# Two attentions in a fused two-layer kernel: both heads of a pair in one step, unsplit scores on half the rows each

## The chip, the cores and the metric

One core of a Trainium2 chip runs one program. The metric is the device time of one execution in microseconds (us), here the median of three runs. The engines are named as in the profile: PE is TensorE's matmul side, PEld its weight loads, DVE is VectorE, ACT is ScalarE, POOL is GpSimd, SP is the engine whose queue issues most of the DMAs.

## The reference, cut to what matters

Two layers follow each other on a sequence of 1024 tokens of width 1024, all in fp32. Each layer projects the tokens, runs several mixers, merges them and ends in an MLP. Each layer has one attention among its mixers:

```python
# layer 1, "fox": 8 heads of 64
for blk in range(L // Q_BLOCK):                       # 8 blocks of 128 queries
    q0 = blk * Q_BLOCK; kend = q0 + Q_BLOCK
    s = jnp.einsum('bqhd,bkhd->bhqk', q[:, q0:kend], k[:, :kend]) * scale
    s = s + cum[:, :, q0:kend, None] - cum[:, :, None, :kend]
    s = jnp.where(k_pos[None, :] <= q_pos[:, None], s, NEG_INF)
    outs.append(jnp.einsum('bhqk,bkhd->bqhd', jax.nn.softmax(s, axis=-1), v[:, :kend]))
# layer 2, "band": 4 heads of 64, chunks of 64 queries, each with the chunk itself and 8 chunks to its left
s = einsum(q, k of the band) * scale + rel_bias[dist];  o = softmax(s) @ v of the band
```

## The kernel before

Almost all of the arithmetic is large products: a weight tile of 128x128 against the activations, 128x1024. Weights and activations are split into a high part in fp32r and a remainder (`w_hi`, `w_lo`, `act_hi`, `act_lo`), and a tile takes six matmuls of 128x512 in fp32r (L322): three products of parts for two halves. Eight tiles are a unit. At the start of a unit ACT casts the next unit's weights (L278), POOL forms the remainder (L282), and when a row of eight tiles is done, DVE evicts it (L609) and SP stores it to DRAM (L611).

The mixers run inside these products. Class `Woven` holds a generator of tiles; `point(n)` in the mixer's code lets it emit as many tiles as the mixer's progress is worth, so that PE's queue holds product tiles between the mixer's own matmuls. `w.again(points, kept)` says over how many points the tiles that are left (but `kept`) are to be spread. For fox these are 384 - 137 = 247 tiles over 8*28+11 = 235 points, for band 143 tiles over 4*28+12 = 124 points. Every engine works through its queue in the order in which the code emits it.

`attention` is used by both. It goes head by head, and in each head over eight query blocks n; a step is one query block of one head. For fox the keys of block n are the first 128(n+1); for band they are 128(n+1) up to n=3 and 640 from n=4. A step does this:

- Scores (L818): q has been cast to fp32r (`qh`, L735) with a remainder `ql` (L736). k lies twice in `ks`: its high part on partitions 0 to 63, its remainder on 64 to 127 (L741, L742), since both halves of `raw_qk` hold the head. Two fp32r matmuls with all 128 rows, `qh` and `ql` against `ks`, so give the score of a head for up to 512 keys. They write `wide`, two PSUM banks.
- DVE adds the bias while it reads `wide` (`add_bias`: L884 and L886 in fox, L920 in band), takes the row maximum (L832) and negates it (L833). ACT takes the exponential with the row sum (L836).
- One step later DVE inverts the sum (L767) and ACT scales the row (L768).
- Two steps later PE transposes the probabilities in groups of up to four blocks into `bank[0]` (L638), and ACT copies each group out (L642). The even head's go to `pe`, which holds a whole head; the odd head's go to `pt`, and right behind them the product with the values follows for both heads (L786), fp32 with 64 columns of the array for each head. So there are 32 groups of L786 in fox and 16 in band. Three buffers of scores `s[:, t % 3]` hold the steps under way.
- `values` transposes v once for each pair (L751), `gather` copies four blocks of output (L794).

`fetch(h + 1)` is issued when head h begins. In fox the bias row of a head is a row of `fox_cum` broadcast over all partitions (`fx_cb`, 512 KB in SBUF, double-buffered, L859), and POOL makes the masked diagonal blocks `fx_own` out of it (L873). A short convolution (`short_conv`) takes up DVE with one instruction each step.

Other mixers of the kernel use fp32 matmuls, unsplit. Three of them matter here. L373 (`row_sums`) multiplies 128 rows and 128 columns by 512: four matmuls in the code. L1244 and L1289 have 64 rows each, two of them on partitions 0 to 63 and then two on 64 to 127, and the two halves write different PSUM banks:

```python
for g in range(2):
    rows_g = slice(S5_P * g, S5_P * (g + 1))
    for c in (RE, IM):
        nc.tensor.matmul(ps[g][:, o:o + CH], cl[rows_g, pr, c, 1:, :]..., state[rows_g, c, pr, :], ...)
```

L1289 loads 128 columns of weights, L1244 16. Both stream 128 columns.

Of the kernel before, what the change touches and what calls it, by code (L numbers as in the profile page):

```python
# [9 lines left out]
P = 128  # L10
# [117 lines left out]
def _build(nc, ctx, t, out):  # L128
# [38 lines left out]
    qk_in = Count(sem("qk_in"))  # L167
# [523 lines left out]
    def attention(heads, tiles, src, rows, stored, mixed, row0, head_bias, add_bias, name, beside, first_queue=nc.sync):  # L691
# [8 lines left out]
        halves = src.rearrange("b (h p) n -> (b h) p n", h=2)  # L700
        with ExitStack() as at:
            raw_qk, raw_v = sb(at, name + "x", [P, 2, L]), sb(at, name + "v", [P, L])
            qh, ql, ks = (sb(at, name + n, [P, 2, L], F32R) for n in ("qh", "ql", "ks"))
            vt = sb(at, name + "vt", [P, NT, P])
            bias, bias_in, bias_fixed = head_bias(at)
            keys = [(k1 - k0) // P for q0, k0, k1 in tiles]
            s, pe = sb(at, name + "s", [P, 3, L]), sb(at, name + "pe", [P, sum(keys), P])
            pt, o, st = sb(at, name + "pt", [P, NT, P]), sb(at, name + "o", [P, L]), sb(at, name + "st", [P, 3, 2])

            arrived, bias_ready, split, scores, biased, values_in, weighed = {}, {}, {}, {}, {}, {}, {}  # L710
            v_read = {}

            def fetch(h):

                queue = SP if h else first_queue
                if h:
                    SP.wait_ge(*split[h - 1])
                for n in range(3):
                    queue.wait_ge(*stored[rows[n] + h // 2])
                for n in range(2):  # L720
                    for half in range(2):
                        arrived[h] = qk_in.mark(queue.dma_start(raw_qk[half * HD:(half + 1) * HD, n, :],
                                                             halves[h + 2 * rows[n]]))
                if h % 2 == 0:
                    if h:
                        SP.wait_ge(*v_read[h - 2])
                    v_in.mark(queue.dma_start(raw_v[:], src[h // 2 + rows[2]]))
                if h > 1:
                    SP.wait_ge(*biased[h - 2])
                bias_in(h)  # L730

            def prepare_q(h):

                sl = h % 2
                a_q = A.mark(A.after(arrived[h], scores.get(h - 2)).copy(qh[:, sl, :], raw_qk[:, 0, :]))  # L735
                V.mark(V.after(a_q).tensor_tensor(ql[:, sl, :], raw_qk[:, 0, :], qh[:, sl, :].bitcast(F32), ALU.subtract))  # L736

            def prepare_k(h):

                sl = h % 2  # L740
                a_k = A.mark(A.after(arrived[h], scores.get(h - 2)).copy(ks[:, sl, :], raw_qk[:, 1, :]))  # L741
                split[h] = V.mark(V.after(a_k).tensor_tensor(ks[HD:P, sl, :], raw_qk[HD:P, 1, :],  # L742
                                                             ks[HD:P, sl, :].bitcast(F32), ALU.subtract))
                bias_ready[h] = bias_fixed(h)

            def values(h, copied):

                for j0 in (0, 4):
                    PE.after(v_in.last(), copied, *(() if h else entered))
                    for j in range(4):  # L750
                        last = nc.tensor.transpose(bank[0][:, j * P:(j + 1) * P], raw_v[:, (j0 + j) * P:(j0 + j + 1) * P],  # L751
                                                   ident[:])
                    ready = PE.mark(last)
                    v_read[h] = ready
                    copied = A.mark(A.after(ready, weighed.get(h - 1)).copy(
                        vt[:, j0:j0 + 4, :], bank[0][:].rearrange("p (j n) -> p j n", j=4)))
                    if j0 == 0:
                        point()
                values_in[h + 1] = copied
                return copied  # L760

            pv_done, turned, state = {}, [], {"copied": None, "o_read": None, "scores_read": None}

            def scaled(t, h, n, k0, nk, e):

                sum_, w = st[:, t % 3, 1:2], nk * P
                v = V.mark(V.after(e).reciprocal(sum_, sum_))  # L767
                return A.mark(A.after(v).activation(s[:, t % 3, 0:w], s[:, t % 3, 0:w], ACT.Copy, scale=sum_))  # L768

            def turn(t, h, n, k0, nk, e):  # L770

                few, even = nk <= 4, pe[:, sum(keys[:n]):sum(keys[:n + 1]), :]
                point((1.5 if few else 1) + (2 if n == 0 else 0))
                if t == 0:
                    PE.after(*settled)
                state["copied"] = transposes(pt[:, 0:nk, :] if h % 2 else even, lambda j: s[:, t % 3, j * P:(j + 1) * P], nk, P,
                                             e, free=state["copied"], after=lambda: point(1.5 if few else 1))
                turned.append(state["copied"])
                if h % 2 == 0:
                    point(0.5)  # L780
                    return
                PE.after(state["copied"], values_in[h], state["o_read"])
                for j in range(nk):
                    for x, p in enumerate((even, pt)):
                        mine = slice(x * HD, (x + 1) * HD)
                        last = nc.tensor.matmul(bank[1][mine, n % 4 * P:(n % 4 + 1) * P], vt[:, k0 // P + j, mine],  # L786
                                                p[:, j, :], start=j == 0, stop=j == nk - 1)
                pv_done[t] = weighed[h] = PE.mark(last)

            def gather(t, h, n):  # L790

                if h % 2 == 0 or n % 4 != 3:
                    return
                state["o_read"] = V.mark(V.after(pv_done[t], out_in.get(h // 2 - 1)).tensor_copy(  # L794
                    o[:, n // 4 * HALF:(n // 4 + 1) * HALF], bank[1][:]))
                if n == NT - 1:
                    SP.wait_ge(*V.last())
                    out_in[h // 2] = stores[0].mark(SP.dma_start(mixed[h // 2 + row0], o[:]))

            out_in = {}  # L800
            fetch(0)
            point(5)
            prepare_q(0)
            prepare_k(0)
            point(3)
            exped, ready_p = None, None
            for t, (h, n) in enumerate((h, n) for h in range(heads) for n in range(NT)):
                q0, k0, k1 = tiles[n]
                w, sl = k1 - k0, t % 3
                if n == 0:  # L810
                    if h + 1 < heads:
                        fetch(h + 1)
                    aside = beside(h)
                PE.after(split[h], state["scores_read"])
                for c in range(0, w, HALF):
                    e = min(w, c + HALF)
                    for q in (qh, ql):
                        last = nc.tensor.matmul(wide[:, c:e], q[:, h % 2, q0:q0 + P], ks[:, h % 2, k0 + c:k0 + e],  # L818
                                                start=q is qh, stop=q is ql)
                scores[h] = ready = PE.mark(last)  # L820
                if t == 0:
                    point(3)
                if ready_p:
                    turn(*ready_p)
                drained = ready_p
                if exped:
                    ready_p = (*exped[:-1], scaled(*exped))
                sc = s[:, sl, 0:w]
                V.after(ready, bias_ready[h], turned[t - 3] if t > 2 else None, *(settled if t == 2 else ()))
                state["scores_read"] = add_bias(h, n, sc, wide[:, 0:w], bias[:, h % 2, :], q0, k0, k1)  # L830
                biased[h] = V.last()
                V.mark(V.then().reduce_max(st[:, sl, 0:1], sc, AX.X))  # L832
                x = V.mark(V.then().tensor_scalar(st[:, sl, 0:1], st[:, sl, 0:1], -1.0, None, ALU.mult))  # L833
                if drained:
                    gather(*drained[0:3])
                x = A.mark(A.after(x).activation(sc, sc, ACT.Exp, bias=st[:, sl, 0:1], accum_out=st[:, sl, 1:2]))  # L836
                exped = (t, h, n, k0, w // P, x)
                if n == 3 and h % 2 == 0:
                    state["copied"] = values(h, state["copied"])
# [12 lines left out]
    def fox(stored):  # L852
# [28 lines left out]
        def add_bias(h, n, sc, psum, cb, q0, k0, k1):  # L881
# [8 lines left out]
            elif n < 2 and h:  # L890
                mask(h, n + 6)
# [1337 lines left out]
```

## Time and profile before

| | |
|---|---|
| median of 3 runs | 3460.83 us (3458.84 to 3464.54) |
| the profiled execution, device time | 3463.03 us |
| its span, first to last instruction | 3461.3 us |
| PE busy | 3366.4 us, 97% of the span |
| DVE, ACT, POOL busy | 38%, 27%, 27% |
| fox, first to last instruction of its own on PE | 313.7 to 762.6 us |
| band, the same | 1822.0 to 2065 us |

A busy share of PE counts a matmul from its start to its modelled end, and matmuls overlap, so it is high wherever matmuls follow each other closely. What a piece of work costs PE is read from the starts: how much later the products behind it begin than they would without it.

### The profile page before, as it was taken

Reading aid. Unit: us, or ns where it says so; the run is one execution under the profiler, and the core shown is the slowest. Engines: PE = TensorE matmul, PEld = TensorE weight load, DVE = VectorE, ACT = ScalarE, POOL = GpSimd, SP = SyncE. Lnnn points to the kernel's source line nnn. Section 1 sums busy time; section 2 is a strip of 40 time slices with the busy share of each in tenths; the row PEclk is TensorE's granted clock in tenths of the full one; section 3 lists DMA queues with packets and bytes.
Section 4 is the critical chain, followed back from the end, with each engine's and each line's share of the span. In section 5 each row is a group of like instructions: output and inputs, shape, how many; then the busy total and the mean of one; then the engine's idle time right before and its main releaser. Section 6 shows DMA issues by size and latency. Waiting matters only on the chain. (4 is left out here: it accounts for less than half of the span.)

```text
span 3461.3 us, 40933 instructions
## 1 busy us (share of the span) xinstructions
PE 3366.4 (97%) x16184; PEld 2739.9 (79%) x16184; DVE 1311.0 (38%) x1631; ACT 944.6 (27%) x1248; POOL 940.3 (27%) x507
## 2 busy tenths in 40 slices
PE   8999999999999999999999999999999999999997
PEld 6788888777877888888867777787878688888886
DVE  6852455434244131313143427654461521121123
ACT  3213444444232111111233332313342411111112
POOL 2212222213332222222421124231254222122125
PEclk9999999999999999999999999999999999999998
DMA  3435444235411111111233222213362211111113
GB/s 129 159 94 159 129 151 149 95 115 184 146 63 65 49 49 49 48 49 47 93 125 118 96 101 101 80 68 144 136 213 97 79 48 49 48 48 49 49 52 130
DMA packets 101603, 333.43 MB, mean 96 GB/s; under 512 B 11920, under 2 KB 21520, under 8 KB 101328
## 3 DMA queue, kind: packets, MB, share of 16 engines
q1 hardware_dynamic: 100432, 327.95, 28.3%
q10 hardware_dynamic: 1040, 3.67, 0.3%
q8 instruction: 90, 1.47, 0.2%
q14 instruction: 41, 0.34, 0.0%
HBM read 249.06 MB, written 85.52 MB: 97 GB/s over the span
## 5 line engine op out<-in xcount | busy, mean ns | idle before, releaser
L282 POOL TENSOR_TENSOR w_lo<-w_raw,w_hi 128x1024 fp32r<-128x1024 f32 (+1 forms) x304 | 694.8, 2289 | 2348.8 <-ACT w_hi L278 2299.7
L322 PE MATMUL pair<-act_hi,w_hi 128*128 128x512 f32 x2976 | 942.8, 398 | 6.5 <-DVE f1v L2000 1.5
L322 PE MATMUL pair<-act_lo,w_hi 128*128 128x512 f32 x2976 | 920.9, 391 | 0.0
L322 PE MATMUL pair<-act_hi,w_lo 128*128 128x512 f32 x2976 | 919.6, 390 | 0.0
L322 PEld LDWEIGHTS pair<-act_hi,w_lo 128*128 128x128 f32 x2976 | 559.6, 188 | 119.8
L322 PEld LDWEIGHTS pair<-act_lo,w_hi 128*128 128x128 f32 x2976 | 559.6, 188 | 119.3
L322 PEld LDWEIGHTS pair<-act_hi,w_hi 128*128 128x128 f32 x2976 | 539.9, 189 | 111.9 <-issue 10.0
L278 ACT CAST w_hi<-w_raw 128x1024 fp32r<-128x1024 f32 x274 | 287.4, 1049 | 848.4 <-PE pair L322 802.2
L609 DVE TENSOR_TENSOR p<-pair,rs 128x1024 f32<-128x1024 f32 x100 | 122.2, 1222 | 406.4 <-PE pair L322 406.3
L1943 DVE TENSOR_TENSOR f2v<-pair,rs 128x1024 f32<-128x1024 f32 x42 | 51.4, 1225 | 333.1 <-PE pair L322 333.1
L322 PE MATMUL pair<-f1hl,w_hi 128*128 128x512 f32 x480 | 147.8, 389 | 0.0
L322 PE MATMUL pair<-f1hh,w_hi 128*128 128x512 f32 x480 | 147.8, 389 | 0.0
L322 PE MATMUL pair<-f1hh,w_lo 128*128 128x512 f32 x480 | 147.7, 389 | 0.0
L441 PE MATMUL pair<-act_hi,w_hi 128*128 128x512 f32 x192 | 87.1, 453 | 26.6 <-DVE act_lo L545 13.7
L1937 DVE TENSOR_TENSOR f1v<-pair,rs 128x1024 f32<-128x1024 f32 x30 | 36.7, 1224 | 186.2 <-PE pair L322 186.2
L1932 ACT CAST f1hh<-f1v 128x1024 f32 x30 | 31.5, 1050 | 276.1 <-DVE f1v L1938 276.1
L322 PEld LDWEIGHTS pair<-f1hl,w_hi 128*128 128x128 f32 x480 | 90.1, 188 | 18.7
L322 PEld LDWEIGHTS pair<-f1hh,w_hi 128*128 128x128 f32 x480 | 90.1, 188 | 18.7
L322 PEld LDWEIGHTS pair<-f1hh,w_lo 128*128 128x128 f32 x480 | 90.1, 188 | 18.7
L1969 DVE TENSOR_TENSOR f1y<-f1y,pair 128x1024 f32 x22 | 26.9, 1221 | 201.3 <-PE pair L322 201.3
L322 PE MATMUL pair<-f2hh,w_lo 128*128 128x512 f32 x328 | 101.0, 389 | 0.0
L322 PE MATMUL pair<-f2hh,w_hi 128*128 128x512 f32 x328 | 101.0, 389 | 0.0
(486 smaller groups left out, 4042.8 us busy)
## 6 DMA issues: line engine op xcount, KB each, us to landing
w_raw<-in_stream SPq DMA_DIRECT2D x275, 512.0 KB, 3.6
proj<-p SPq DMA_DIRECT2D x101, 512.0 KB, 2.6
m2g<-proj SPq DMA_DIRECT2D x32, 512.0 KB, 4.8
m1g<-proj SPq DMA_DIRECT2D x16, 512.0 KB, 3.5
x<-f1y SPq DMA_DIRECT2D x16, 512.0 KB, 2.6
act_lo<-x SPq DMA_DIRECT2D x16, 512.0 KB, 6.9
foxx<-proj SPq DMA_DIRECT2D x28, 256.0 KB, 5.7
fx_cb<-fox_cum SPq DMA_DIRECT2D x8, 512.0 KB, 7.5
```

Of the source, the lines that this page charges most:

```text
L278: nc.scalar.copy(whi[:, slot, :], raw[:, slot, :]).then_inc(s_whi, 1)
L282: last = nc.gpsimd.tensor_tensor(wlo[:, slot, at:at + n], raw[:, slot, at:at + n], whi[:, slot, at:at + n].bitcast(F32), ALU.subtract)
L322: last = nc.tensor.matmul(out_pair[:, h * HALF:(h + 1) * HALF], wt, a[:, h * HALF:(h + 1) * HALF], start=k == 0 and n_pass == 0, stop=k == ...
L441: last = nc.tensor.matmul(out, wt, a[:, half], start=k == 0 and n_pass == 0, stop=k == self.tiles - 1 and n_pass == 2)
L609: done = read(V.after(ready, stored).tensor_tensor(buf[:, slot, :], psum[:], rs[:], ALU.mult))
L1932: a = A.mark(A.after(mark).copy(hi, x[:, s, :]))
L1937: a = read(V.then(ready).tensor_tensor(x[:, s, :], psum[:], rs[:], ALU.mult))
L1943: v = read(V.then(ready).tensor_tensor(x[:, o, :], psum[:], rs[:], ALU.mult))
L1969: done = read(V.after(ready).tensor_tensor(dst, dst, psum[:], ALU.add))
```

## The change

A step is now one query block of both heads of a pair; fox has 32 steps and band 16. q and k of the pair are loaded as they lie in DRAM, one head on partitions 0 to 63 and one on 64 to 127, and go to PE as they are, in fp32, with 64 rows for each head; the casts and remainders of q and k (L735 to L742) are gone. Each head's scores of up to 512 keys go to its own half of `wide`. A query block with more than 512 keys so has two groups of scores, the second of which (`scores(i, n, HALF)`) waits until DVE has read the first. Transposes and the product with the values follow one step behind the scores instead of two, with two buffers. In fox the own (diagonal) rows and the bias rows of a pair are loaded separately, and there is one buffer for each head of a pair: those of the next pair are loaded when the last reader in this pair is through. In band the biases of all four heads are loaded at the start. The points become 4*57+13 = 241 for fox and 2*57+13 = 127 for band; the tiles are the same.

```diff
+            def fetch(i):
+                queue = SP if i else first_queue
...
+                if i > 1:
+                    SP.wait_ge(*scored[i - 2])
                 for n in range(2):
+                    arrived[i] = qk_in[i % 2].mark(queue.dma_start(qk[:, i % 2, n, :], src[i + rows[n]]))
...
-            def prepare_q(h):
-                a_q = A.mark(A.after(arrived[h], scores.get(h - 2)).copy(qh[:, sl, :], raw_qk[:, 0, :]))
-                V.mark(V.after(a_q).tensor_tensor(ql[:, sl, :], raw_qk[:, 0, :], qh[:, sl, :].bitcast(F32), ALU.subtract))
-            def prepare_k(h):
...
+            def scores(i, n, c):
+                q0, k0, k1 = tiles[n]
+                w = min(HALF, k1 - k0 - c)
+                PE.after(arrived[i], state["scores_read"])
+                for x in range(2):
+                    head = slice(x * HD, (x + 1) * HD)
+                    last = nc.tensor.matmul(wide[:, x * HALF:x * HALF + w], qk[head, i % 2, 0, q0:q0 + P],
+                                            qk[head, i % 2, 1, k0 + c:k0 + c + w], start=True, stop=True)
+                scored[i] = ready = PE.mark(last)
+                for x in range(2):
+                    state["scores_read"] = add_bias(i, n, x, c, c + w, s[:, t % 2, x, :], wide[:, x * HALF:x * HALF + w],
+                                                    V.after(ready, turned.get(t - 2), *(settled if t < 2 else ())))
+            def turn(t, x, j0, m, ready):
+                PE.after(ready[x], state["bank"], *(settled if t == 0 else ()))
+                for j in range(m):
+                    last = nc.tensor.transpose(bank[0][:, j * P:(j + 1) * P], s[:, t % 2, x, (j0 + j) * P:(j0 + j + 1) * P],
+                                               ident[:])
+                turned[t] = PE.mark(last)
+                state["bank"] = A.mark(A.after(turned[t]).copy(
+                    pt[:, x, j0:j0 + m, :], bank[0][:, 0:m * P].rearrange("p (j n) -> p j n", j=m)))
+            def groups(n):
+                return [(x, j0, min(4, nk - j0)) for x in range(2) for j0 in range(0, nk, 4)]
...
+            for t, (i, n) in enumerate((i, n) for i in range(pairs) for n in range(NT)):
                 q0, k0, k1 = tiles[n]
+                w, total = k1 - k0, 8 if k1 - k0 > HALF else 6
...
+                scores(i, n, 0)
+                parts = groups(before[1]) if before else [None, None]
+                for g, part in enumerate(parts):
+                    if part:
+                        turn(t - 1, *part, ready)
+                    if g == 1 and w > HALF:
+                        scores(i, n, HALF)
+                    if g == (2 if len(parts) == 4 else int(w > HALF)):
+                        for x in range(2):
+                            V.mark(V.then().reduce_max(sm, sc, AX.X))
+                            exps[x] = V.mark(V.then().tensor_scalar(sm, sm, -1.0, None, ALU.mult))
+                        exps[0] = A.mark(A.after(exps[0]).activation(... ACT.Exp ...))
+                        next(aside, None)
+                    point(total / len(parts))
+                if before:
+                    weigh(*before)
+                if n == 0:
+                    values(i)
+                exps[1] = A.mark(A.after(exps[1]).activation(... ACT.Exp ...))
+                ready = []
+                for x in range(2):
+                    v = V.mark(V.after(exps[x]).reciprocal(sm, sm))
+                    ready.append(A.mark(A.after(v).activation(... ACT.Copy, scale=sm)))
+                if before:
+                    gather(*before)
+                next(aside, None)
+                bias_ahead(i, n)
+                if n == 2 and i + 1 < pairs:
+                    fetch(i + 1)
+                before = i, n
+            for part in groups(before[1]):
+                turn(t, *part, ready)
+                point(2)
+            weigh(*before)
+            gather(*before)
# fox
+            def rows(i):
+                for x in range(2):
+                    here[i] = bias_load[i % 2].mark(SP.dma_start(cb[:, x, :], fox_cum[2 * i + x].partition_broadcast(P)))
+            def ahead(i, n):
+                if n == 0 and i:
+                    SP.wait_ge(*read[i - 1, NT - 1, 1])
+                    own_rows(i, 1, edge)
+                    rows(i)
+                if n < NT - 1:
+                    mask(i, n + 1)
+                elif i + 1 < pairs:
+                    SP.wait_ge(*read[i, NT - 2, 1])
+                    own_rows(i + 1, 0, slice(0, (NT - 1) * P))
+                    mask(i + 1, 0)
+            def add(i, n, x, c, e, sc, psum, vector):
+                left, q0 = min(e, n * P), n * P
+                if left > c:
+                    v = V.mark(V.after(here[i]).scalar_tensor_tensor(sc[:, c:left], psum[:, 0:left - c], HD ** -0.5,
+                                                                     cb[:, x, c:left], ALU.mult, ALU.subtract))
...
-            w.again(FOX_HEADS * 28 + 11, 2 * KT)
+            w.again(FOX_HEADS // 2 * 57 + 13, 2 * KT)
-                w.again(BAND_HEADS * 28 + 12, 32 * KT)
+                w.again(BAND_HEADS // 2 * 57 + 13, 32 * KT)
```

## Rows read from the trace of the kernel before

**Rows 1.** The page, busy time of PE over the whole span.

```profile
PE 3366.4 (97%) x16184; PEld 2739.9 (79%) x16184; DVE 1311.0 (38%) x1631; ACT 944.6 (27%) x1248; POOL 940.3 (27%) x507
```

**Rows 2.** Windows: stretch, its length, busy time of each engine, clock, DMA.

```profile
313.70:762.60 448.90, 442.65 (x2519) 357.69 (x2517) 206.63 (x383) 188.93 (x341) 107.05 (x88) 1.00 0.37 121
1806.00:1822.00 16.00, 12.39 (x55) 9.94 (x53) 2.50 (x3) 4.05 (x4) 4.21 (x5) 0.96 0.64 185
1822.00:2065.00 243.00, 238.00 (x1276) 191.16 (x1276) 85.71 (x163) 87.85 (x172) 47.94 (x43) 0.99 0.30 95
```

**Rows 3.** Waits of PE in fox: us in total, times, longest.

```profile
PE wide L818 <- DVE foxs L886: 3.0, 4, 1.1
```

**Rows 4.** Timeline of PE around two score groups of fox: start, duration, work.

```profile
353.78 0.39 PE L818 MATMUL wide<-foxks,foxqh 128*128 128x512 f32 x1
...
354.68 0.62 PE L322 MATMUL pair<-act_hi,w_hi 128*128 128x512 f32 x2
...
360.37 0.63 PE L322 MATMUL pair<-act_hi,w_lo 128*128 128x512 f32 x2
360.84 0.22 PE L818 MATMUL wide<-foxks,foxqh 128*128 128x128 f32 x1
...
361.01 0.68 PE L322 MATMUL pair<-act_hi,w_hi 128*128 128x512 f32 x2
361.52 0.62 PE L322 MATMUL pair<-act_lo,w_hi 128*128 128x512 f32 x2
```

**Rows 5.** Timeline of PE at fp32 matmuls with 128 rows (L373).

```profile
2355.86 3.59 PE L373 MATMUL wide<-gm_vt,ones 128*128 128x512 f32 x8
2358.89 1.03 PE L322 MATMUL pair<-act_hi,w_hi 128*128 128x512 f32 x2
2359.76 0.62 PE L322 MATMUL pair<-act_lo,w_hi 128*128 128x512 f32 x2
```

**Rows 6.** Timeline of PE at fp32 matmuls with 64 rows, 128 columns (L1289).

```profile
221.41 0.62 PE L322 MATMUL pair<-act_lo,w_hi 128*128 128x512 f32 x2
221.86 0.61 PE L322 MATMUL pair<-act_hi,w_lo 128*128 128x512 f32 x2
222.41 2.16 PE L1289 MATMUL bank<-s_state,s_first 64*128 64x128 f32 x32
224.50 0.72 PE L322 MATMUL pair<-act_hi,w_hi 128*128 128x512 f32 x2
225.06 0.63 PE L322 MATMUL pair<-act_lo,w_hi 128*128 128x512 f32 x2
```

**Rows 7.** Timeline of PE at fp32 matmuls with 64 rows, 16 columns (L1244).

```profile
207.41 0.63 PE L322 MATMUL pair<-act_hi,w_lo 128*128 128x512 f32 x2
207.97 1.93 PE L1244 MATMUL wide<-s_first,s_b 64*16 64x128 f32 x32
209.84 0.73 PE L322 MATMUL pair<-act_hi,w_hi 128*128 128x512 f32 x2
210.40 0.62 PE L322 MATMUL pair<-act_lo,w_hi 128*128 128x512 f32 x2
```

**Rows 8.** DMA issues in fox: count, size, median us from issue to landing.

```profile
fx_cb<-fox_cum SPq DMA_DIRECT2D x8, 512.0 KB, 7.5
```

**Rows 9.** Timeline of PE at the start of band.

```profile
1822.04 0.47 PE L818 MATMUL wide<-bandks,bandqh 128*128 128x128 f32 x1 [3.65 <-DVE bandks L742]
...
1823.48 1.05 PE L322 MATMUL pair<-act_lo,w_hi 128*128 128x512 f32 x2
1824.34 1.05 PE L322 MATMUL pair<-act_hi,w_lo 128*128 128x512 f32 x2
```

**Rows 10.** Lines by form in fox, ACT and DVE: count, busy us, mean ns.

```profile
L836 ACT ACTIVATE foxs<-foxs,foxst 128x256 f32<-128x256 f32 x8 | 4.0, 503 | 2.3 <-DVE foxst L833 2.1
L836 ACT ACTIVATE foxs<-foxs,foxst 128x1024 f32<-128x1024 f32 x8 | 9.1, 1144 | 4.1 <-DVE foxst L833 4.1
L886 DVE SCALAR_TENSOR_TENSOR foxs<-wide,fx_own 128x128 f32<-128x128 f32 x64 | 17.9, 280 | 1.7 <-POOL fx_own L864 1.6
L832 DVE TENSOR_REDUCE foxst<-foxs 128x1 f32<-128x256 f32 x8 | 3.4, 420 | 0.3
```

More of the change, by code:

```diff
@@ L1 @@
+import itertools
 import math
@@ L699, in attention @@
         NT = L // P
-        halves = src.rearrange("b (h p) n -> (b h) p n", h=2)
         with ExitStack() as at:
-            raw_qk, raw_v = sb(at, name + "x", [P, 2, L]), sb(at, name + "v", [P, L])
-            qh, ql, ks = (sb(at, name + n, [P, 2, L], F32R) for n in ("qh", "ql", "ks"))
+            qk, raw_v = sb(at, name + "x", [P, 2, 2, L]), sb(at, name + "v", [P, L])
             vt = sb(at, name + "vt", [P, NT, P])
[L705 to L717, printed above, removed]
+            bias_first, bias_ahead, add_bias = head_bias(at)
@@ L720, in fetch @@
                 for n in range(2):
[L721 to L729, printed above, removed]
@@ L746, in values @@
-            def values(h, copied):
+                    arrived[i] = qk_in[i % 2].mark(queue.dma_start(qk[:, i % 2, n, :], src[i + rows[n]]))
+                if i:
+                    SP.wait_ge(*v_read[i - 1])
+                v_in.mark(queue.dma_start(raw_v[:], src[i + rows[2]]))
+            def values(i):
                 for j0 in (0, 4):
-                    PE.after(v_in.last(), copied, *(() if h else entered))
-                    for j in range(4):
-                        last = nc.tensor.transpose(bank[0][:, j * P:(j + 1) * P], raw_v[:, (j0 + j) * P:(j0 + j + 1) * P],
+                    PE.after(v_in.last(), state["bank"], *(() if i else entered))
+                    for j in range(j0, j0 + 4):
+                        last = nc.tensor.transpose(bank[0][:, (j - j0) * P:(j - j0 + 1) * P], raw_v[:, j * P:(j + 1) * P],
@@ new lines, in weigh @@
+            def weigh(i, n):
+                q0, k0, k1 = tiles[n]
+                nk = (k1 - k0) // P
+                PE.after(state["bank"], copied[i], state["o_read"])
+                for j in range(nk):
+                    for x in range(2):
+                        head = slice(x * HD, (x + 1) * HD)
+                        last = nc.tensor.matmul(bank[1][head, n % 4 * P:(n % 4 + 1) * P], vt[:, k0 // P + j, head],
+                                                pt[:, x, j, :], start=j == 0, stop=j == nk - 1)
+                weighed[i] = PE.mark(last)
@@ L801, in attention @@
+            def groups(n):
+                q0, k0, k1 = tiles[n]
+                nk = (k1 - k0) // P
+                return [(x, j0, min(4, nk - j0)) for x in range(2) for j0 in range(0, nk, 4)]
             fetch(0)
+            bias_first()
             point(5)
[L803 to L807, printed above, removed]
+            before, ready = None, None
@@ L820, in attention @@
[L820 to L839, printed above, removed]
@@ L840, in attention @@
-                if n == 4 and h + 1 < heads:
-                    prepare_q(h + 1)
-                if n == 5 and h + 1 < heads:
-                    prepare_k(h + 1)
-                next(aside, None)
-            turn(*ready_p)
-            gather(*ready_p[0:3])
-            ready_p = (*exped[:-1], scaled(*exped))
-            point(1)
-            turn(*ready_p)
-            gather(*ready_p[0:3])
+                    aside = itertools.chain(beside(2 * i), beside(2 * i + 1))
+                scores(i, n, 0)
@@ L894, in fox @@
+            return first, ahead, add
         with ExitStack() as at:
-            attention(FOX_HEADS, [(n * P, 0, (n + 1) * P) for n in range(8)], proj1, (Q_, K_, V_), stored, mixed1, 8,
-                      head_bias, add_bias, "fox", short_conv(at, stored), nc.scalar)
+            attention(pairs, [(n * P, 0, (n + 1) * P) for n in range(8)], proj1, (Q_, K_, V_), stored, mixed1, 8,
+                      head_bias, "fox", short_conv(at, stored), nc.scalar)
     def band(beside, stored):
+        pairs = BAND_HEADS // 2
```

161 lines of the change are left out of this document (66 added, 95 removed).

## The prediction

> **What bounds the kernel now.** I read the page first. PE is busy 97% of the span and no other engine more than 38% (PEld, the weight loads, runs beside PE) [rows 1], so the question for every edit is what it does to PE. Then I read the windows over the two attentions. In fox PE stands idle for 448.90 - 442.65 = 6.25 us, in band for 243.00 - 238.00 = 5.0 us, and just before band's first score for 16.00 - 12.39 = 3.6 us [rows 2]. Everything else, 11.3 us apart, is PE working through its queue: the product tiles that are woven in cover the softmax chain. The largest group of waits on PE in fox is only 3.0 us, four waits for DVE to empty `wide` [rows 3]. So ACT and DVE work that the change removes (the casts and remainders of q and k, four instructions a head) is hidden work. It can give back no more than a part of those 11.3 us. What counts is what the new matmuls cost PE, read from starts in the timeline.
>
> **Pitch of a pass.** A product pass of 512 columns starts 0.228 us after the one before: two from 221.41 to 221.86 [rows 6]. That is the clock's upper level, 2.4 GHz, which the window shows as 1.00. An fp32 matmul costs more. L373 is four matmuls in the code and eight records in the trace, so one fp32 matmul is two passes. From 2355.86 to 2359.76 lie those eight and two product passes: (3.90 - 0.46) / 8 = 0.43 us for a pass of 512 columns [rows 5]. An fp32 matmul of 512 columns therefore takes 0.86 us, four times 1/2.4 GHz a column, with nothing added before or behind. In the sums below a pass is 0.43/512 = 0.00084 us a column in fp32 and half of that in fp32r.
>
> **Scores before.** Four fp32r passes of 512 columns (one head, 1024 keys) take 354.68 - 353.78 = 0.90 us [rows 4], 0.225 each, with no cost of switching. Two of 128 columns take 361.52 - 360.37 = 1.15 less four product passes, 0.91: 0.24 us, which is 0.13 more than their columns. For a pair of heads of fox that is 2 heads x 2 passes x 4608 keys (128 times 1 to 8) x 0.225/512 = 8.1 us plus four groups of 128 keys x 0.13, 8.6 us; four pairs, 34.5 us. Band has 3840 keys a head: 6.75 + 10 x 0.13 = 8.05 us a pair, 16.1 us for two. Before: 50.6 us.
>
> **Scores after, the columns.** Each head is now one fp32 matmul, two passes of 0.00084 us a column, with 64 rows. No score of the kernel before is of this form, but L1289 and L1244 are: fp32, 64 rows, alternate halves of the partitions, different banks. L1289's 32 records of 128 columns last 2.16 us in all [rows 6]; one after the other they would take 32 x 0.107 = 3.4 us. They fit 16 slots of 0.107, that is 1.7 us: the two halves run side by side. So I take both heads of a pair for the price of one: 2 passes x 4608 x 0.00084 = 7.74 us a pair, 31.0 in fox; 2 x 3840 x 0.00084 = 6.45 a pair, 12.9 in band. Together 43.9 us. This alone would be 6.7 us less than before.
>
> The Trainium skill, "TensorE: Matmul & The Clock Gate", section "The mechanism", says that matmuls start and end strictly in the order of the program, even on different row groups. The first rival takes that up from the rows.
>
> **Scores after, the switch.** A group with 64 rows costs PE more than its slots. L1289: from 221.86 to 225.06 are 3.20 us, less four product passes 2.29, less 16 slots 0.57 us too much [rows 6]. L1244 in the same way: 2.99 - 0.91 - 1.72 = 0.36 us [rows 7]. The two differ in the columns of weights they load, 128 and 16. The new scores load 128, but their passes are mostly long enough to hide the second load, which 128-column slots aren't (L1289's excess includes that). So 0.57 for the groups of 128 keys down to about 0.4 for the longer ones; I take 0.435 a group on the mean, with 0.36 and 0.57 as bounds. Below nothing is excluded: every group in this form in the trace has the excess. The groups are 12 a pair (one for each of eight blocks, a second for the four with more than 512 keys): 48 in fox, 24 in band, 72 x 0.435 = 31.3 us (25.9 to 41.0). Scores after: 43.9 + 31.3 = 75.2 us. The term is 75.2 - 50.6 = **+24.6 us** (+19.2 to +34.3).
>
> **Transposes, values, output.** The number and size of transposes (L638), of products with the values (L786), of their groups and of the switches to 64 columns for them are the same: 0 us. Tiles are the same number too, 247 and 143; spread over 241 points instead of 235 they come to 1.03 a point.
>
> **Lag of one step.** With every step the scaled probabilities must be ready when PE reaches the next step's first transpose. Take a small step: behind the last transposes stand three points, 3.1 tiles of six passes, 4.2 us; then the values of the block before and the next scores, 1.7 us or more. ACT's second exponential and both scalings stand in the queue behind the last copy, 0.5 us each at 256 keys [rows 10], so they are through inside the tiles. Only where a unit of weights begins at the very end of the tiles does the cast get in ahead of them, and that costs under 1 us. In the largest step, 1024 keys, two points (2.8 us) and then the values and the next scores stand over a copy, an exponential of 1.14 us [rows 10] and a scaling that I take as equally long, some 3.1 us. I take 2 us for all steps together (0 to 6). What is queued behind these waits on PE is the next tiles, nobody else.
>
> **What goes.** Of the 11.3 us of idle [rows 2], the waits for `wide` at 256 to 384 keys, the ones at v's transposes and the tails, where two whole steps were turned without enough tiles between, lose their cause: -9 us. The 3.6 us before band stay. There PE waited for q and k, then for their splitting [rows 9]. The splitting (about 4 us) goes, but three points of tiles (3.4 tiles, 4.7 us) that stood ahead of the first scores now stand behind them, so PE reaches them as much earlier and waits for the load itself. The half clock that followed (two product passes 0.86 us apart instead of 0.46, level 1.2 GHz [rows 9]) I take to stay too: 0 us.
>
> **What comes: bias rows at the change of pair in fox.** This edit moves a load from a head ahead to the moment of use. `rows(i)` goes out at the end of the pair's first step. SP must first pass the store of the output, which waits for `gather`, and that for the second exponential, which stands behind the copies of v. I put the issue of the second bias row at 3.3 us after PE starts the scores of step 1, my estimate from the order of the queues, with the store and three other issues ahead of it. A bias row lands 7.5 us after its issue [rows 8], so at about 11. DVE stands at the first bias add of step 1 until then. Then four adds of 0.28, a maximum of 0.42 and its negation bring the first exponential to 12.7, 13.3 when done [rows 10]. ACT has the copy of the second head's transposes behind that exponential. PE comes to the product with the values, which needs that copy, after 0.8 of scores, 0.6 of transposes and six points (8.5 us), at 9.9 us, and waits until 13.7. That is 4 us at each of three changes of pair: **+12 us** (0 if the rows leave and land 4 us earlier, 20 if the clock falls after each wait as it did before band, where the mean clock of 0.99 over 243 us [rows 2] stands for some 5 us at half clock, 2.5 us lost).
>
> **Sum.** 24.6 + 2 - 9 + 12 = +29.6 us; against the profiled execution's 3463.0 that is 3492.6. The profiled execution lies 2.2 us above the median of the runs, so by the median 3460.8 + 29.6, **3490 us**, 0.9% slower. Its own range is 3478 to 3504: the switch between its bounds or the bias waits between theirs, not both at their ends.
>
> **Rivals.**
> Passes start strictly in order. Then of first head pass 1, pass 2, second head pass 1, pass 2 only the middle two overlap: three slots instead of two, half of 43.9 more, +22 us, 3512. For it: the program order. Against: in L1289 four records of one half come ahead of four of the other, in order that would take 24 slots, 2.6 us, and they took 2.16 [rows 6]. The Trainium skill's rule above is this rival; by it the time would be 3512, and this trace speaks against it.
> No overlap at all: another 22 us, 3534. Against it is the same row, more strongly.
> One more stall: the softmax chain no longer fits into one step and PE waits in each of the 48 steps, by 0.5 us, 24 us in all: 3514. For it is the lag; against it the slack worked out above.
> No measurable change: the switch at its lower bound and no wait for the bias, 19.2 + 2 - 9 = +12, and some 5 to 9 us more won at band's start, should the load be there when PE asks for it: 3464 to 3468.
> Faster: the switch costs nothing for passes of 512 columns. Then the scores are 6.7 us cheaper, with 9 us of idle gone and 2 us new 3447 by the median, if the bias rows come in time. The point from which it decides is a switch of 0.09 us: 72 x 0.09 - 6.7 - 9 + 2 = -7. For it: an fp32 group with 128 rows costs no switch [rows 5]. Against: rows 6 and 7.
>
> **How the numbers follow.** The forecast 0.58, strict order 0.13, no overlap 0.07, a stall in each step 0.06, no change 0.08, faster 0.08. The range leaves out no overlap, faster and half of no change, 0.19: 3466 to 3520. By 0.2% (7 us, about what a measurement of this kernel tells from no change): faster 0.08, same 0.08, slower 0.84.
>
> **What the changed profile would show.** Score groups with 64*128 shapes whose two heads' records start within 0.02 us of each other, passes 0.43 us apart at 512 columns; a group of 512 keys for both heads costing 1.3 us between products where two heads cost 0.9 before. If the second head's records start a pass later, strict order holds. PE waiting at L786's successor for ACT's copy at three places some 10 us into the second step of a pair, with DVE waiting there for the bias DMA. No other waits of PE above 1 us inside the attentions. Fox's stretch longer by about 20 us and band's by about 7. The prediction is wrong if the switch behaves otherwise for long passes than for short ones, since both rows that price it have 128 columns.

## The result and the profile after

The median went from 3460.83 us to 3479.74 us (five runs, 3474.50 to 3480.45): the ratio is 1.005, 95% interval 1.0035 to 1.0064, slower by 18.9 us. The forecast was slower, 3490 us with a range of 3466 to 3520. So the direction was right, and the loss is two thirds of the 29.6 us that were forecast.

The profiled execution is the fastest of the five, 3474.50 us, 11.5 us above that of before; the other four took 3478.9 to 3480.5 us at a mean granted clock of 0.992 instead of 0.994, which is 0.002 x 3478 / 0.5 = 14 us more at the lower level, 7 us lost. Where the sums below go by the trace, they are held against what happened inside the two attentions.

The page of the changed kernel, busy time over the span (before: [rows 1]):

```profile
PE 3375.4 (97%) x16184; PEld 2717.1 (78%) x16184; DVE 1275.0 (37%) x1645; ACT 919.7 (26%) x1224; POOL 938.5 (27%) x514
```

ACT lost 25 us of work and DVE 36 us, and the time went up: as in [rows 1], PE alone decides. The windows over the attentions (stretch, length, busy time of PE, PEld, DVE, ACT, POOL, clock, DMA; before: [rows 2]):

```profile
308.12:778.71 470.59, 457.47 (x2534) 348.12 (x2534) 183.85 (x393) 176.02 (x327) 102.26 (x95) 0.99 0.33 117
1832.52:2077.90 245.38, 243.93 (x1300) 187.86 (x1300) 79.29 (x171) 82.74 (x167) 48.27 (x43) 0.99 0.24 88
```

Fox's stretch is 21.7 us longer and band's 2.4 us, but both now begin three points of tiles (3 or 4 tiles) earlier. So I number the product tiles in both traces and measure from the start of a tile to the start of a later one. From tile 128 (260.36 us before, 258.57 after) to tile 400 (762.56 and 778.91) fox takes 18.2 us more; from tile 1120 (1804.63 and 1820.96) to tile 1296 (2119.28 and 2132.66) band takes 3.0 us less. That is +15.2 us. The difference of the two executions is 11.5, so outside the attentions the changed kernel was 3.7 us shorter: the code is the same there, but some 8 us less of it ran at half clock, which is 4 us lost less.

PE around a score group that stands between tiles, 512 keys of both heads; the three transposes ahead of it have the tiling of the product tiles. (Tiling is here the rows and columns of the array that a matmul uses, which the profile writes as 128*128, 64*128 or 128*64; a switch is what a change of it costs PE.)

```profile
402.25 0.62 PE L324 MATMUL pair<-act_hi,w_lo 128*128 128x512 f32 x2
402.71 0.49 PE L755 MATMUL bank<-ident,foxs 128*128 128x128 f32 x3
403.13 1.13 PE L744 MATMUL wide<-foxx 64*128 64x512 f32 x4
404.19 0.73 PE L324 MATMUL pair<-act_hi,w_hi 128*128 128x512 f32 x2
404.76 0.62 PE L324 MATMUL pair<-act_lo,w_hi 128*128 128x512 f32 x2
```

Four records (two passes for each head) last 1.13 us. One after the other they would need 4 x 0.43 = 1.7. The price is read as in [rows 6]: from 402.25 to 404.76 are 2.51 us, less four product passes 1.60, less 0.34 for three transposes 1.26, less 2 x 0.43 a switch of **0.40 us**. It was 0.41 for 128 keys and 0.40 for 256 and 384 in the same way.

PE around a score group that stands right behind the product with the values (L769):

```profile
349.49 0.61 PE L324 MATMUL pair<-act_hi,w_lo 128*128 128x512 f32 x2
350.04 0.88 PE L769 MATMUL bank<-foxpt,foxvt 128*64 128x128 f32 x12
350.85 1.13 PE L744 MATMUL wide<-foxx 64*128 64x512 f32 x4
351.90 0.66 PE L755 MATMUL bank<-ident,foxs 128*128 128x128 f32 x4
352.32 0.70 PE L324 MATMUL pair<-act_hi,w_hi 128*128 128x512 f32 x2
352.86 0.63 PE L324 MATMUL pair<-act_lo,w_hi 128*128 128x512 f32 x2
```

The group is the same size, 512 keys of both heads. From 349.49 to 352.86 are 3.37 us, less four product passes 2.46, less 0.45 for four transposes 2.01. The product with the values costs 1.01 by itself (it stands alone in the second experiment below), so the scores cost 1.00, and less their 0.86 the switch is **0.14 us**. The prediction priced it at 0.435 everywhere.

The first change of pair in fox. The score group of the new pair's step 1, which needs the bias rows, in PE's timeline:

```profile
430.98 0.70 PE L744 MATMUL wide<-foxx 64*128 64x256 f32 x4
```

The load of this pair's bias rows (L851), issued after that, in the timeline of SP's queue:

```profile
433.09 0.93 SPq L851 DMA_DIRECT2D fx_cb<-fox_cum  x2
```

What then waited, in the timeline of all engines (in brackets the idle time ahead and what ended it):

```profile
439.84 0.29 DVE L890 SCALAR_TENSOR_TENSOR foxs<-wide,fx_cb 128x128 f32<-128x128 f32 x1 [7.59 <-DMA fx_cb<-fox_cum]
...
441.40 0.51 ACT L810 ACTIVATE foxs<-foxs,foxst 128x256 f32<-128x256 f32 x1 [9.15 <-DVE foxst L809]
...
441.91 1.03 ACT L280 CAST w_hi<-w_raw 128x1024 fp32r<-128x1024 f32 x1
...
442.84 0.26 ACT L758 COPY foxpt<-bank 128x128 f32<-128x128 f32 x1
...
443.15 0.44 PE L769 MATMUL bank<-foxpt,foxvt 128*64 128x128 f32 x4 [2.86 <-ACT foxpt L758]
```

This is the chain that was forecast, link by link: scores, the load issued too late, DVE waiting for it, the exponential behind DVE, the copy behind the exponential, PE behind the copy. The waits of PE in fox (before: [rows 3]):

```profile
PE bank L769 <- ACT foxpt L758: 8.0, 3, 2.9
PE bank L755 <- ACT foxs L825: 3.6, 6, 0.7
PE bank L730 <- ACT foxvt L733: 0.8, 1, 0.8
```

Three such waits. Of the others none is above 0.8 us. Three of the six behind L825 (0.69, 0.51 and 0.56 us) stand right behind the three long waits, so PE was idle for 8.0 + 1.8 = 9.8 us at the changes of pair. Behind each it then ran at the lower level of the clock for 3.41 us, which these windows show:

```profile
444.60:448.01 3.41, 2.88 (x8) 2.40 (x9) 3.33 (x6) 1.25 (x3) 2.76 (x3) 0.50 0.79 251
560.60:564.01 3.41, 3.21 (x9) 2.63 (x10) 3.30 (x8) 1.48 (x5) 0.00 (x0) 0.51 0.02 5
676.70:680.11 3.41, 3.41 (x10) 2.73 (x10) 1.56 (x6) 0.57 (x3) 2.13 (x3) 0.50 0.60 202
```

The start of band (before: [rows 9]):

```profile
1832.52 0.49 PE L744 MATMUL wide<-bandx 64*128 64x128 f32 x4 [3.24 <-DMA bandx<-proj]
...
1834.95 1.05 PE L324 MATMUL pair<-act_hi,w_hi 128*128 128x512 f32 x2
1835.81 1.05 PE L324 MATMUL pair<-act_lo,w_hi 128*128 128x512 f32 x2
```

PE now waits for the load itself, for 3.24 us instead of 3.65, and then runs with two passes 0.86 us apart (1.2 GHz), as before.

### The profile page after: what moved, and what is told of

It reads as the page before. It is cut to its first block and busy times, and to the rows that moved or that the text cites. A ratio compares the mean times of both kernels' runs of the same rounds, so it can differ in the third digit from the quotient of the medians.

```text
span 3472.8 us, 40847 instructions
## 1 busy us (share of the span) xinstructions
PE 3375.4 (97%) x16184; PEld 2717.1 (78%) x16184; DVE 1275.0 (37%) x1645; ACT 919.7 (26%) x1224; POOL 938.5 (27%) x514
## 5 line engine op out<-in xcount | busy, mean ns | idle before, releaser
L324 PE MATMUL pair<-f2hl,w_hi 128*128 128x512 f32 x328 | 101.0, 389 | 0.0
```

Of the source, the lines that this page charges most:

```text
L324: last = nc.tensor.matmul(out_pair[:, h * HALF:(h + 1) * HALF], wt, a[:, h * HALF:(h + 1) * HALF], start=k == 0 and n_pass == 0, stop=k == ...
```

## The experiments

The first four ran on one chip beside the kernel before (3461.12 us, 23 runs), the other four on another (3461.34 us, 27 runs). The changed kernel wasn't run again beside them: where a run is compared with its 3479.74 us, or a run of the second four with e1, which is of the first, the two times come from different sets of runs. The kernel before has medians of 3460.83, 3461.12 and 3461.34 us in the three sets. What is quoted as the number of a kernel is its median.

**e1: load the bias rows earlier.** In the changed kernel (cut; the readers of `cb` get the same index):

```diff
-            cb, own = sb(at, "fx_cb", [P, 2, L]), ...
+            cb, own = sb(at, "fx_cb", [P, 2, 2, L]), ...
             def ahead(i, n):
                 if n == 0 and i:
                     SP.wait_ge(*read[i - 1, NT - 1, 1])
                     own_rows(i, 1, edge)
-                    rows(i)
+                if n == 3 and i + 1 < pairs:
+                    if i:
+                        SP.wait_ge(*read[i - 1, NT - 1, 1])
+                    rows(i + 1)
```

> The changed kernel with one edit: fx_cb has two buffers for each head and the bias rows of the next pair are loaded during the fourth step of this pair. Theory (the waits at the three changes of pair cost about 13.5 us, as the blocks there exceed their usual cost by 4.3 to 4.7 us each, half clock included): 13 to 16 us faster than the changed kernel, about 3465, and no PE wait above 1 us left behind L755 and before L769. Rival (the waits cover something else that is then late, or the extra DMA traffic costs as much): less than 5 us faster, 3475 or more.

Measured: 3464.95 us (ten runs), 14.8 us faster than the changed kernel, ratio to before 1.001 (1.000 to 1.002). By the differences to before it is 18.9 - 3.8 = 15.1 us. The three waits are gone; the largest that are left of PE's waits in fox:

```profile
PE bank L755 <- ACT foxs L825: 1.9, 3, 0.7
PE bank L769 <- ACT foxpt L758: 0.8, 1, 0.8
```

So the late bias rows cost some 15 us, as much as four fifths of the whole loss. The two traces say the same, tile by tile: at the three changes of pair (tiles 229 to 232, 287 to 290, 345 to 348) the changed kernel falls behind e1 by 5.0, 4.6 and 5.0 us, **14.6** together (at the first, tile 229 starts at 438.77 in the one and 436.85 in the other, tile 232 at 449.49 and 442.55). Of these 9.8 are idle, and 4.8, or 1.6 each, go to the half clock behind the waits.

**e2 and e3: part the score groups from their neighbours.** Both are e1 with one point of tiles moved from the end of the step (the diff shows both edits, each run has one of them):

```diff
+                if before:
+                    point(1)          # e2: here, between the values and the scores
                 scores(i, n, 0)
+                if before:
+                    point(1)          # e3: here instead, between the scores and the transposes
...
-                    point(total / len(parts))
+                    point(total / len(parts) - (1 if before and g == len(parts) - 1 else 0))
```

> The kernel of e1 with one point of tiles moved from the end of each step to between the product with the values and the next scores, 46 places. Theory A (each change of the array's tiling costs PE some 0.13 to 0.2 us, and back to back groups save one): one change more at each place, a group of values and scores costs 0.375 + 0.40 instead of about 0.50, so 0.27 x 46 = 12.6 us slower than e1. Rival B (the group was cheap because the transposes follow it, not because the values precede it): no difference from e1 within 3 us.

> The kernel of e1 with one point of tiles moved from the end of each step to between the scores and the transposes behind them. Theory A (number of changes of tiling; transposes and product tiles are the same tiling): as many changes as before, 0 us against e1, within 3 us. Rival B (transposes hide the way out of the 64-row form): 0.2 to 0.27 us at each of 46 places, 9 to 12.6 us slower than e1.

Measured: e2 3472.98 us (eight runs), 8.0 above e1; e3 3469.97 us (ten runs), 5.0 above e1. Theory A had said 12.6 and 0, within 3; rival B 0, within 3, and 9 to 12.6. So neither is right in both, and e3 lies between them. In e2's timeline the two groups stand apart:

```profile
348.00 0.61 PE L324 MATMUL pair<-act_hi,w_lo 128*128 128x512 f32 x2
348.55 0.88 PE L769 MATMUL bank<-foxpt,foxvt 128*64 128x128 f32 x12
349.35 0.72 PE L324 MATMUL pair<-act_hi,w_hi 128*128 128x512 f32 x2
349.92 0.63 PE L324 MATMUL pair<-act_lo,w_hi 128*128 128x512 f32 x2
350.39 0.62 PE L324 MATMUL pair<-act_hi,w_lo 128*128 128x512 f32 x2
350.94 1.13 PE L744 MATMUL wide<-foxx 64*128 64x512 f32 x4
352.00 0.66 PE L755 MATMUL bank<-ident,foxs 128*128 128x128 f32 x4
352.41 0.70 PE L324 MATMUL pair<-act_hi,w_hi 128*128 128x512 f32 x2
352.95 0.40 PE L324 MATMUL pair<-act_lo,w_hi 128*128 128x512 f32 x1
```

The values cost 349.92 - 348.00 - 0.91 = 1.01, the scores 352.95 - 350.39 - 0.91 - 0.45 = 1.20, together 2.21 where the same work back to back cost 2.01. That is 0.20 a place. In the second step of a pair, v's transposes stand between the values and the scores anyway, so of the 46 places 40 are parted anew: 8.0 us, what was measured. In e3:

```profile
364.50 0.61 PE L324 MATMUL pair<-act_hi,w_lo 128*128 128x512 f32 x2
365.04 1.09 PE L769 MATMUL bank<-foxpt,foxvt 128*64 128x128 f32 x16
366.07 1.13 PE L744 MATMUL wide<-foxx 64*128 64x512 f32 x4
367.12 0.73 PE L324 MATMUL pair<-act_hi,w_hi 128*128 128x512 f32 x2
367.70 0.62 PE L324 MATMUL pair<-act_lo,w_hi 128*128 128x512 f32 x2
```

Values and scores cost 3.20 - 0.91 = 2.29; in the changed kernel the place with the same sizes and the transposes behind it costs 2.67, less 0.45 for these 2.22. So parting scores from transposes costs 0.06 to 0.07 a place, 3 us in all, a third of what parting them from the values costs. The remaining 2 us of e3 I can't place as surely; its profiled execution has one new wait of 2.7 us for a copy (PE goes on at 575.92) with half clock behind it, where a cast got in ahead. Theory A holds in its mechanism, not in its size: PE pays for each change of tiling, 0.40 for a group by itself (in and out), and a group in a second tiling directly behind one in a first saves 0.2 where 0.27 had been taken. What rival B names exists too, and is worth 0.06 to 0.07 a place.

**e4: both heads on one half of the rows.** e1 with one line changed; it computes the first head's scores twice:

```diff
-                    head = slice(x * HD, (x + 1) * HD)
+                    head = slice(0, HD)
```

> The kernel of e1 with both score matmuls of a group reading the first head's half of the partitions, so it computes the first head's scores twice (that part of the result is changed); columns, rows, banks and everything behind it stay. Theory (the halves run side by side): twice the pass time, +43.9 us against e1. Rival (two passes overlap only partly in the changed kernel): half of that, 22 us, or less.

Measured: 3508.56 us, 43.6 above e1. The group of 512 keys:

```profile
410.05 0.62 PE L324 MATMUL pair<-act_hi,w_lo 128*128 128x512 f32 x2
410.51 0.49 PE L755 MATMUL bank<-ident,foxs 128*128 128x128 f32 x3
410.92 1.98 PE L744 MATMUL wide<-foxx 64*128 64x512 f32 x4
```

1.98 us instead of 1.13, two passes more. Nothing but the half of the partitions is different, so on two halves the passes overlap fully. The rival of a partial overlap had said 22 us or less.

**e5 and e6: tiles ahead of band's first scores.** e5 is e1 and e6 is the kernel before, each with the wait at the start of band filled:

```diff
-            point(5)
+            point(5 if name == "fox" else 8)      # e5; in e6 9
...
-                w.again(BAND_HEADS // 2 * 57 + 13, 32 * KT)
+                w.again(BAND_HEADS // 2 * 57 + 16, 32 * KT)      # e6: BAND_HEADS * 28 + 16 instead of 12
```

> The kernel of e1 (3465) with three points of tiles moved ahead of band's first scores, spread over 130 points instead of 127, where PE waits 3.9 us for the load of q and k and runs at half clock after it. Theory: the wait and the half clock go, 4 to 6 us, about 3460, level with the kernel before. Rival (the tiles that are moved are missing further on, or half clock falls elsewhere): no change against e1.

> The kernel before with the same edit alone: four points more of tiles ahead of band's first score, over 128 points instead of 124. PE waited there 3.65 us and ran some 5 us at half clock. Theory: 4 to 6 us faster than before, about 3456. Rival: no change, as for e5.

Measured: e5 3459.90 us (11 runs), 5.1 below e1, ratio to before 0.9995 (0.9986 to 1.0004), level with it. e6 3453.75 us (11 runs), ratio to before 0.9974 (0.9965 to 0.9983), faster than both kernels of this study. e6's windows at the start of band and over it, to be held against [rows 2]:

```profile
1806.00:1822.00 16.00, 16.00 (x72) 13.26 (x71) 4.50 (x4) 4.06 (x4) 5.66 (x5) 1.00 0.75 224
1822.00:2065.00 243.00, 239.79 (x1298) 193.42 (x1297) 83.64 (x165) 90.41 (x174) 52.58 (x46) 1.00 0.31 101
```

PE is busy for all of the 16 us and the clock stays at 1.00. It gained 7.6 us, some 2 us more than expected. The wait of 3.65 us and half of the 4.9 us at half clock behind it (1822.04 to 1827.0 in the trace of before) make 6.1 of it; the rest isn't placed.

**e7: the form of the scores alone.** The kernel before, one head a step, three score buffers, lag of two; only the scores are unsplit fp32 with 64 rows. Since both halves of the partitions hold the head there, half of the keys goes to each (cut; the casts are gone and q and k have two buffers):

```diff
-                        last = nc.tensor.matmul(wide[:, c:e], q[:, h % 2, q0:q0 + P], ks[:, h % 2, k0 + c:k0 + e],
-                                                start=q is qh, stop=q is ql)
+                at0 = HALF - w // 2
+                for x in range(2):
+                    part = slice(x * HD, (x + 1) * HD)
+                    last = nc.tensor.matmul(wide[:, at0 + x * (w // 2):at0 + (x + 1) * (w // 2)],
+                                            raw_qk[part, h % 2, 0, q0:q0 + P],
+                                            raw_qk[part, h % 2, 1, k0 + x * (w // 2):k0 + (x + 1) * (w // 2)],
+                                            start=True, stop=True)
```

> The kernel before with one part of the change alone: scores unsplit in fp32 with 64 rows, here one head at a time, the first half of its keys on one half of the partitions and the second on the other, both in flight together; no casts of q and k; q and k double-buffered; steps, lag of two steps, bias loads and points as before. Theory (what the change costs is its 64-row form): columns 43.9 us, 48 isolated groups x 0.40 and 48 behind the product with the values or v's transposes x 0.2 is 72.7 us instead of 50.6, +22, less 4 to 6 us at band's start, where the splitting goes: +16, about 3477. Rival (the loss lies in the shorter lag and the two-head step): within 5 us of before.

Measured: 3479.90 us (four runs), 18.6 above before, ratio 1.0052 (1.0037 to 1.0067). A group by itself, 1024 keys of one head:

```profile
353.28 0.63 PE L322 MATMUL pair<-act_hi,w_lo 128*128 128x512 f32 x2
353.84 1.13 PE L811 MATMUL wide<-foxx 64*128 64x512 f32 x4
354.90 0.73 PE L322 MATMUL pair<-act_hi,w_hi 128*128 128x512 f32 x2
355.46 0.62 PE L322 MATMUL pair<-act_lo,w_hi 128*128 128x512 f32 x2
```

It costs 2.18 - 0.91 = 1.27 us where the fp32r group of the kernel before costs 0.90 [rows 4]. So the form costs as such, with the old steps, the old lag and the old bias loads; the rival, within 5 us of before, falls. In this kernel the number of groups is 96, and 54 of them don't stand right behind the product with the values; in the changed one it is 72 and 32.

**e8: the hidden work put back.** e1 with eight dummy instructions a pair, in steps 3 to 6:

```diff
+                if n in (3, 4, 5, 6):
+                    a = A.mark(A.then(V.last()).copy(spare[:, 0, :], qk[:, i % 2, n % 2, :]))
+                    V.mark(V.then(a).tensor_tensor(spare[:, 1, :], qk[:, i % 2, n % 2, :], spare[:, 0, :], ALU.subtract))
```

> The kernel of e1 with the kind of work put back that the change removed: in each pair four ACT casts of 128x1024 and four DVE subtractions of 128x1024 into a buffer that nobody reads, each pair of them one after the other. Theory (that work was hidden under the tiles): within 3 us of e1, 3465. Rival (ACT and DVE had a share in the time): 5 us or more slower.

Measured: 3465.33 us (ten runs), 0.4 above e1, and the same ratio to before, 1.001. The fox part of it, 16 copies of 1.05 us and 16 subtractions of 1.23 us, is 36 us of work that costs nothing where it stands. It stands in the middle of a pair; at the start of band, where PE waited for the splitting itself, e8 says nothing.

## Why the prediction was right, and where a term was off

**What bounds.** Right. PE decides; the casts and remainders that the change takes from ACT and DVE are worth nothing under the tiles (e8).

**Columns.** Right. Two heads side by side on the two halves cost the time of one: 43.9 us were forecast for all columns, and taking the overlap away cost 43.6 (e4). Both rivals that denied it, strict order of the passes and no overlap, fall. In the changed kernel the four records of the group at 403.13 start at 403.131, 403.138, 403.664 and 403.671, and end within 1.13 us. On one half (e4) they start one after another, 0.43 to 0.53 us apart, so the two that start together belong to different heads: first passes side by side, then second ones. The profile doesn't say which of the two is which head's. The Trainium skill's rule in "TensorE: Matmul & The Clock Gate", section "The mechanism", that matmuls start and end strictly in the order of the program, was taken by the prediction to hold for each pass, and for passes this trace speaks against it. For whole matmuls of the program, of which each is two passes, nothing here speaks against it: the second head's needn't start or end before the first's.

**The switch.** This is the term that was mis-sized. The prediction took 0.435 us for all 72 groups, 31.3 us, with 25.9 to 41.0 as bounds. In the trace, 24 second groups (`scores(i, n, HALF)`), 2 first ones and the 6 that stand behind v's transposes and tiles cost 0.40 each, close to it, while the 40 right behind the product with the values cost 0.14: 12.8 + 5.6 = 18.4 us, below the lower bound. The term is then 43.9 + 18.4 - 50.6 = +11.7 us instead of +24.6. The step that failed is not the price of a group but that it was applied to groups that share a change of tiling with their neighbour; the only rows with such groups stood between product tiles. e2 shows it: parting them costs 0.20 a place. It also failed in its guess that passes of 512 columns make the switch cheaper; it is 0.40 for each length.

**The bias rows at the change of pair.** Right in mechanism and place: +12 us forecast, 14.6 in the profiled execution, 14.8 by e1. That the size is near is in part luck. The forecast was three waits of 4 us and no loss of clock; there were 9.8 us idle, and the half clock added 4.8. Counted from PE's scores of the step (430.98), the load was forecast to be issued at 3.3 and to land at 11; it was issued by 3 and landed at 8.9. PE was to reach the product with the values at 9.9 and to wait until 13.7; it came at 9.3 and went on at 12.2. That the cast of weights would get in between the exponential and the copy (1.0 us) wasn't foreseen, and made up for part of the earlier landing. The half clock behind it was kept as a possibility; it came in each of the three places of the profiled execution.

**Lag, what goes, band's start.** Forecast +2, -9 and 0, together -7. Taken by difference inside the attentions, 15.2 - 11.7 - 14.6 = -11.1. Of these the traces show 7.6. The idle time of PE in the two windows, without that at the changes of pair, is 3.3 and 1.5 us where it was 6.3 and 5.0 [rows 2], 6.5 less; the wait at band's start is 0.4 shorter; and 3.4 us of half clock stand behind it instead of 4.9, 0.7 saved. The other 3.5 us I can't place, and no run tests them. The lag of one step costs next to nothing: all waits for scaled probabilities in fox are 3.6 us, 1.8 of them behind the late bias rows and gone in e1, and two of 0.7 in second steps of a pair. So the rival of a stall in each step falls. Band's start stayed nearly as it was, for the reason given: the splitting went, and the scores came up against the load. For band as a whole the forecast was 7 us longer and it is 3.0 shorter, by tiles: its 11 switches of 0.40 and 13 of 0.14 cost 6.2 us where 24 x 0.435 = 10.4 were forecast, and some 6 of the 11.1 us lie in band.

**Sum.** The terms 11.7 + 14.6 - 11.1 give the +15.2 of the profiled execution, but only because the last is what is left over; the first two are measured. The median says +18.9. The 3.7 between them I put to the half-clock stretches, which the four other runs have more of; that wasn't tested, as only one trace of the kernel exists. Had the switch been 18.4, the forecast would have been 29.6 - 12.9 = +16.7. That the forecast comes out within 11 us has a share of luck: it had 12.9 us too much for the switch and took off 4.1 too few for what goes, and against that stand 2.6 too few for the bias rows and the 3.7 outside the terms.

What stays open: the two-head step with the scores split as before. By the terms it should be the fastest (e5 less 11.7 us, some 3448, an estimate), but the split operands of two pairs are 48 KB a partition where e5's q and k take 16, beside fox's other buffers. It wasn't tried.

## What to carry to other kernels

On a kernel whose one engine is never idle, price a new form of its instruction with all that it costs at its edges, and by neighbours: a matmul group in another tiling cost 0.40 us between product tiles here, whatever its length, and 0.14 behind a group that had already left that tiling. Where an edit merges two units of work and halves their buffers, look first at the loads that were issued one unit ahead: they are now issued when they are needed, and here that cost some 15 of the 18.9 us, while the new form cost 11.7 and what the change saved paid for most of that. The gain that was to be had lay in neither kernel's attention but in the wait ahead of it (e6: 7.6 us for four points of tiles).

## What the runs showed of the hardware that was not expected

The switch of tiling does not add up: values alone 0.36 us over their columns (1.01 less six slots of 0.108), scores alone 0.34 to 0.40, both in a row 0.50. Parting the scores from transposes, which have the tiling of the product tiles, still costs 0.06.

Each of the four idle stretches of PE of 2.4 to 3.2 us in the two attentions of the changed kernel drew 3.4 us at 1.2 GHz behind it in the profiled execution. At the three changes of pair the waits so cost 14.6 us for 9.8 us of idle time, half as much again.
